# An encoder layer whose residual additions are done by GpSimd instead of VectorE

## What is computed

```python
def ffn_half(x, g_pre, g_post, w_gu, w_dn):
    return x + 0.5 * rmsnorm(swiglu(rmsnorm(x, g_pre), w_gu, w_dn), g_post)

    x = ffn_half(x, g[0], g[1], w_ffn_gu[l, 0], w_ffn_dn[l, 0])
    ...
    mix = jnp.concatenate([...], axis=-1) @ w_out[l]
    x = x + rmsnorm(mix, g[3])
    qc = (rmsnorm(x, g[4]) @ w_cq[l]).reshape(B, T, HC, DHC)
    oc = cross_attend(qc, mem_k, mem_v).reshape(B, T, HC * DHC) @ w_co[l]
    x = x + rmsnorm(oc, g[5])
    x = ffn_half(x, g[6], g[7], w_ffn_gu[l, 1], w_ffn_dn[l, 1])
```

## Time and profile before

| | us |
|---|---|
| median of 3 runs | 2715.04 |
| lowest and highest of them | 2713.97, 2716.89 |
| the profiled execution, whole | 2721.04 |
| its span, first to last instruction | 2719.3 |
| TensorE busy | 2588.2 (95% of the span) |
| VectorE busy | 1233.6 (45%) |
| ScalarE busy | 927.9 (34%) |
| GpSimd busy | 64.1 (2%) |

### The profile page before, as it was taken

How to read it: one execution, slowest core, us unless ns; L and a number is a source line. 1 busy time by engine, 2 the same in 40 slices (tenths; PEclk the granted TensorE clock), 3 DMA queues, 4 the chain that set the end, 5 groups by cost and what they waited for, 6 DMA issues and landing times.

```text
span 2719.3 us, 48175 instructions
## 1 busy us (share of the span) xinstructions
PE 2588.2 (95%) x19513; PEld 2462.7 (91%) x19513; DVE 1233.6 (45%) x2123; ACT 927.9 (34%) x1680; POOL 64.1 (2%) x199
## 2 busy tenths in 40 slices
PE   6999999999998899999999999999999988999998
PEld 6999998996697799999989999989867977999998
DVE  4444325445746554442264442253456656444323
ACT  3222223225643532222242222232356435322221
POOL 1000000001100000000000000000110000000000
PEclk9999999999998999999999999999999889999999
DMA  6223322332023023333223333233311311223321
GB/s 182 85 85 91 92 86 94 115 109 63 30 84 106 24 70 89 89 91 94 71 71 88 90 88 96 80 95 118 114 38 49 106 55 47 78 85 87 97 86 65
DMA packets 383971, 229.80 MB, mean 85 GB/s; under 512 B 6636, under 2 KB 371198, under 8 KB 383840
## 3 DMA queue, kind: packets, MB, share of 16 engines
q1 hardware_dynamic: 378272, 206.59, 25.8%
q0 software_dynamic: 4368, 16.92, 1.8%
q10 hardware_dynamic: 1200, 4.46, 0.4%
HBM read 214.39 MB, written 18.79 MB: 86 GB/s over the span
## 4 chain that ended last, share of the span: by engine, by line
PE 88%; DVE 6%; ACT 3%; DMA 1%; issue 1%; SPq 0%; DVEq 0%; ACTq 0%
PE psum L632 72%; PE psum L607 4%; PE psum L868 4%; PE psum L688 3%; PE psum L887 2%; DVE w_lo L1371 2%; PE psum L889 1%; ACT w_hi L1055 1%; DVE x L1409 1%; PE psum L881 1%; DVE u_lo L1366 1%; PE psum L647 1%; DMA w_raw<-in_w_ffn_gu 0%; DVE y_mix L1406 0%; DVE y_ffn L1406 0%
## 5 line engine op out<-in xcount | busy, mean ns | idle before, releaser
L632 PE MATMUL psum<-u_hi,w_hi 128*128 128x272 f32 x3840 | 816.9, 292 | 27.4 <-DVE w_lo L1371 14.9
L632 PE MATMUL psum<-u_hi,w_lo 128*128 128x272 f32 x3840 | 809.3, 290 | 0.0
L632 PE MATMUL psum<-u_lo,w_hi 128*128 128x272 f32 x3840 | 807.5, 289 | 0.0
L1055 ACT ACTIVATE w_hi<-w_raw 128x1024 fp32r<-128x1024 f32 (+1 forms) x336 | 376.6, 1121 | 1140.0 <-PE psum L632 1061.4
L632 PEld LDWEIGHTS psum<-u_hi,w_hi 128*128 128x128 f32 x3840 | 611.5, 190 | 32.7 <-DVE w_lo L1371 18.0
L632 PEld LDWEIGHTS psum<-u_lo,w_hi 128*128 128x128 f32 x3840 | 612.5, 190 | 0.0
L632 PEld LDWEIGHTS psum<-u_hi,w_lo 128*128 128x128 f32 x3840 | 609.1, 190 | 0.0
L1371 DVE TENSOR_TENSOR w_lo<-w_raw,w_hi 128x1024 fp32r<-128x1024 f32 (+1 forms) x336 | 436.7, 1300 | 352.4 <-ACT w_hi L1055 351.5
L632 PE MATMUL psum<-h_hi,w_hi 128*128 128x272 f32 x1408 | 307.8, 290 | 0.4
L632 PE MATMUL psum<-h_lo,w_hi 128*128 128x272 f32 x1408 | 305.1, 288 | 0.0
L632 PE MATMUL psum<-h_hi,w_lo 128*128 128x272 f32 x1408 | 305.1, 288 | 0.0
(11 more groups left out here) (223 smaller groups left out, 2397.3 us busy)
## 6 DMA issues: line engine op xcount, KB each, us to landing
w_raw<-in_w_ffn_gu SPq DMA_DIRECT2D x176, 512.0 KB, 3.8
w_raw<-in_w_ffn_dn SPq DMA_DIRECT2D x64, 704.0 KB, 4.7
w_raw<-in_w_in SPq DMA_DIRECT2D x48, 512.0 KB, 3.8
w_raw<-in_w_out SPq DMA_DIRECT2D x16, 512.0 KB, 4.1
w_raw<-in_w_ckv SPq DMA_DIRECT2D x16, 512.0 KB, 4.1
bias_tab_dram<-bias_rev_dram POOLq DMA_DIRECT2D x1, 5120.0 KB, 21.6
table<-bias_tab_dram SPq DMA_DIRECT2D x16, 320.0 KB, 3.0
out<-k_nat POOLq DMA_DIRECT2D x4, 1024.0 KB, 5.1
```

The costliest lines, as they stand in the source:

```text
L632: pe_last[0] = pe.matmul(psum[:, bank + part, 0:c1 - c0], w, xx[:, c0:c1], start=s0, stop=s1)
L1055: return act.activation(out, src, ACT.Copy, scale=scale)
```

## The change

DVE keeps the multiplication (line 1406) and loses the wait and the addition behind it (line 1409). GpSimd gets a function add_to_x that waits for each product (y_normed) and adds it into x, and it is called once per update, in program order between GpSimd's other work. x_ready is now incremented by GpSimd. All other waits stand as they were; that of DVE for a complete half of x, ahead of the u_lo blocks, was met by DVE's own addition and is now met by GpSimd's.

```diff
+        def add_to_x(l, st, y):
+
+            q = 4 * l + st + 1
+            for half in range(2):
+                cols = half_of(half)
+                for p in range(4):
+                    pool.wait_ge(y_normed, 8 * (q - 1) + 4 * half + p + 1)
+                    into = x[:, 2 * p:2 * p + 2, cols]
+                    pool.tensor_tensor(into, y[:, 2 * p:2 * p + 2, cols], into, ALU.add).then_inc(x_ready, 1)
...
         for l in range(DEPTH):
+            add_to_x(l, 0, y_ffn)
             store_keys(l, 0, *k_outs[0])
...
+            add_to_x(l, 1, y_mix)
             pool.wait_ge(kv_nat, l * 8 + 4)
...
             pool.wait_ge(mem_stored, l * 32 + 32)
+            add_to_x(l, 2, y_mix)
+            add_to_x(l, 3, y_ffn)
...
                 dve.tensor_tensor(part, part, r, ALU.mult).then_inc(y_normed, 1)
-                dve.wait_ge(y_normed, 8 * (q - 1) + 4 * half + p + 1)
-                into = x[:, 2 * p:2 * p + 2, cols]
-                dve.tensor_tensor(into, part, into, ALU.add).then_inc(x_ready, 1)
                 if between:
                     between(p)
```

## The result

The changed kernel took 2729.16 us, median of 6 runs (2723.93 to 2732.27), against 2714.51 for the kernel before (6 runs, 2713.45 to 2716.89): ratio 1.0052, 95% interval 1.0039 to 1.0064. A second comparison on another occasion gave 2726.16 against 2716.31, ratio 1.0035 [1.0022, 1.0048]. By the medians the change costs 14.7 us in the one and 9.9 us in the other. The forecast was +6.5 us, 2721.5: the direction and the range held, and the size was too small.

The account below looks back on a forecast made before the run. The prediction took TensorE to bound the kernel. Its terms, 0.5 + 3.2 + 1.8 + 2.9 - 1.9 = +6.5 us on a median of 2715.04, gave 2721.5 us; the overall range ran from 2708 to 2738.

Parts of the forecast that it names:

- What bounds the kernel: TensorE, busy 95% of the span; the 46.4 us of moved DVE additions count only where TensorE waits at x's updates.
- P: Time of one two-input addition of 544 elements on GpSimd, taken as 1.25 us, range 1.03 to 1.67.
- Exclusion: GpSimd additions and DVE instructions with two SBUF inputs cannot overlap; the rival without it had 0.25, at 2712.1 us.
- Second halves: Five places, after feed-forward and cross-attention: four GpSimd additions in line, 5.75 us instead of 5.65; +0.5 us in all.
- First halves after feed-forward: Three places: weight cut and sum of squares held by additions, last addition 1.06 us late each; +3.2 us in all.
- Update after the mix: Two places: weight cuts held by additions, 0.6 us late at the second half's start, 0.9 at the last step; +1.8 us.
- After cross-attention: First halves, two places: additions, sums and a cut hold each other, the last addition 1.45 us late each; +2.9 us.
- The end: Last update's second half: x complete as before, but copies out no longer stand behind DVE's additions; -1.9 us.
- TensorE's clock: A lower clock in TensorE's longer gaps would add to any case; no size or chance given.
- The signs named beforehand: GpSimd additions near 1.25 us, cuts and sums held or additions longer, u_hi wait 11.7 to about 18, end 1.9 earlier.
- the forecast's own case: Exclusion holds and one GpSimd addition takes 1.1 to 1.5 us: 2721.5 us, range 2715 to 2733, chance 0.5.

Follow-up runs that it names:

- beside_add: Kernel before, plus GpSimd additions of two unused tiles beside DVE's own in the feed-forward updates; 2733.31 us in one run, before beside it 2715.16.
- beside_set: As beside_add, but GpSimd writes zeros (memset of 128x544) in place of the additions and reads nothing; 2712.93 us in one run, before beside it 2715.16.
- filled pair: tail_fit and after_fit, two kernels with spare TensorE multiplications sized to its idle gaps; 2708.60 and 2720.06 us.
- after_fit: Changed kernel plus spare TensorE multiplications, their number fitted to its waits for u_hi; 2720.06 us, ratio 1.0018 to the kernel before.
- tail_fit: Kernel before with GpSimd adding in the last update's second half alone, plus spare TensorE multiplications fitted to its waits; 2708.60 us, ratio 0.9968.
- unfilled traces: Traces of the kernel before and of the changed kernel, two each, without spare multiplications; spans 2719.3 and 2709.1, then 2726.7 and 2726.0 us.
- tail_only: Kernel before with GpSimd adding in the second half of the last update alone; 2715.71 us against 2716.36, ratio 0.9998.

## Why the prediction was right in direction and short in size

- **What bounds the kernel**: right. Taking 64 instructions from an engine at 45% gained nothing where TensorE did not wait for it, and all that moved lies in the updates of x.
- **P, 1.25 us**: short. Back to back in a second half an addition takes 1.32; the group means are 1.35 and 1.41, with its holds. The affine select and the copy scaled whole gave 1.24 and 1.25; both have one input. By the text's own sensitivity, 4.6 us per 0.1 us of P, a P of 1.32 gives +9.7 and one of 1.35 +11.1: this one size explains most of what was missing.
- **Exclusion**: right, though one copy held for 0.08 us was thin evidence, and some luck was in it. Without it the forecast would have been 2712.1 and on the wrong side. beside_add and beside_set show it apart from the rest.
- **Second halves**: predicted 5.75 us and +0.1 each; measured 6.09 and +0.44, in sum 2.2 for 0.5. Four additions that are 0.07 longer each make 0.3 of that; the text said that this term would be the first to fall.
- **First halves after feed-forward**: mechanism right (the cut held to the end of A1, the sum to the end of A2), size 1.37 for 1.06. Three in sum: 4.1 for 3.2.
- **Update after the mix**: mechanism right, size 1.94 for 0.9 each in the filled pair, so that this term is off by the most, 3.9 for 1.8. The prediction had two holds, on the cuts behind M4 and at the last step. In the trace of after_fit the first two cuts of the second half take 2.23 and 2.05 us and the last 1.55, where the same cuts take 1.22 and 1.23 in tail_fit. The wait for mv_nat rose by 1.0 each; the rest comes before it. In the unfilled traces the same stretch is only 1.0 longer each (32.6 to 34.8 us before), because there other waits vary it.
- **After cross-attention**: 1.42 for 1.45 each. This is luck: with a P of 1.35 the same working gives 1.75.
- **The end**: -1.6 for -1.9 from M0 of the second half, the place of the prediction; four additions that are 0.07 to 0.1 longer each account for it. Counted from the first half it is -1.3, since that half took 8.65 us for 8.36. That is not the additions: it took 8.63 in tail_only, where DVE adds in it, and 8.28 in after_fit.
- **TensorE's clock**: the text said in one sentence that a lower clock would add to any case, and put no term for it in the sum. The stretches give 13.0 us in the filled pair and 12.9 in the unfilled traces; less the 1.3 of the end that is 11.6 to 11.7 for the whole change. The two comparisons have the means of their spans 12.1 and 9.5 us above that of the 88 runs of before, 10.8 together. So the chain alone makes up the loss, and no part is left over that only the clock could explain. Within it the first halves of the feed-forward and cross-attention updates grew by 8.7 unfilled and by 6.9 at full clock, and the mix by 2.0 and 3.9: single stretches move by a microsecond or two with the clock and with the waits around them, the sum hardly does.
- **How much is the clock** stays open. Filling gave 9.0 us to the changed kernel and 8.2 to the other, which makes the clock's share 0.8 with an error of 2. Two other readings do not fit this: among 88 runs of before a mean clock lower by 0.001 goes with 2.2 us more, and on that line 6.6 of the 10.8 us would be clock; and TensorE's busy time rose by 6.6 us. At equal clock the filled pair would then have to lie some 4 apart, and it lies 10.3. An explanation would be that TensorE at 1.2 GHz in a place where DVE or GpSimd sets the pace turns waiting into slow work and costs nothing; that is argued and was not tried.
- **The signs named beforehand**: the wait for u_hi rose to 16.0, not to 18; additions 1.32 apart in a second half; cuts and sums longer by nearly the rest of the running addition; the end 1.6 earlier, not 1.9. All point to the forecast's own case.

## What to carry to other kernels

Before work goes from DVE to GpSimd, look at what DVE does beside it: if those instructions read two operands from SBUF, both engines take turns, and a move that frees 46 us of an engine at 45% busy can cost 10 on the path. Price a chain of instructions on the slower engine at both ends of the guess, since every error in one of them is multiplied by those in line (here 46 additions). Before a remainder is put down to the clock, follow every chain to where the bounding engine is released: here that of the mix's update, beyond its first half, holds 2.8 us that are easily missed. And where the bounding engine waits in many short gaps, look at its clock: filling the gaps with spare multiplications, in a number read from the idle times, gave 0.3% to either kernel.

## What the runs showed of the hardware that was not expected

- A two-input fp32 addition of 128x544 on GpSimd takes 1.32 us back to back. The Trainium skill (GPSIMD Engine Reference, section Elementwise — side-by-side cycle accounting) gives 2.6 cycles per element, which makes an estimate of 1.18 us; the runs have 0.14 more, and the measurement decides.
- GpSimd's memset of 128x544 takes 0.553 us, and the DVE additions and weight cuts of that kernel have the means that they have in before, 0.725 and 1.223 us.
- With two-input work on both sides each holds the other: in beside_add 17 of DVE's 32 additions take 1.11 to 1.15 us, the others 0.72 to 0.73, and GpSimd's 1.62 to 1.91. That kernel lost 18 us in its one run; its work and its waits differ from those of the changed kernel, so the two losses cannot be compared.
- In and behind the updates of x, in which no wait of TensorE for u_hi is longer than 1.1 us before and 2.5 us after, it ran at 1.2 GHz for a part of the time (0.68 to 0.87 in the stretches above). Over the whole span, by the mean granted clock, it was at that level for about 130 and 110 us in the two traces of before (0.976 and 0.980), 136 in both of after (0.975), and 70 and 90 in those of after_fit and tail_fit (0.987 and 0.983).
- The scatter between runs of one kernel is nearly all clock: of the 88 runs of before (2707.7 to 2724.4 us), a straight line in the mean granted clock leaves a standard deviation of 1.6 us.
